# A two-layer attention block on one core: the residual is kept feature-major instead of token-major, and norm, gates and first products follow from that

## What is computed

```python
mod_x = silu(c) @ ada_w[l] + ada_b[l]          # 3*D columns: shift, scale, gate; the same for c_ctx
h  = rmsnorm(x, norm_w) * (1 + scale) + shift  # hc likewise from ctx, with c_ctx's rows
p  = h @ w_in                                  # keys, values, queries, z and g columns
o_m, o_s, o_a = three attentions (latent, windowed, axial) over x and ctx
y  = sum over b of sigmoid(g_b) * ((o_b * silu(z_b)) @ w_o_b)
x  = x + gate * (y @ w_out)                    # ctx likewise, in layer 0 only
...
return rmsnorm(x, final_norm_w)                # after both layers
```

## Time and profile before

| what | us |
|---|---|
| median of 3 runs | 2136.5 |
| profiled execution, its own time | 2135.2 |
| its span | 2133.4 |
| PE busy | 1837.2 (86%) |
| DVE busy | 1210.5 (57%) |
| ACT busy | 889.6 (42%) |
| POOL busy | 602.6 (28%) |
| start until the first projection, PE busy 48.7 | 104.0 |
| merge of layer 0, PE busy 145.6 | 172.8 |
| merge of layer 1, PE busy 79.4 | 93.9 |
| w_out of layer 1 | 46.8 |

### The profile page before, as it was taken

One profiled execution on the slowest core, in us unless ns is written; L12 is line 12 of the kernel. 1 busy time (PEld: TensorE's weight loads), 2 busy tenths in 40 slices (PEclk: granted clock), 3 DMA queues, 4 the chain that ended last, 5 costly groups with the idle time before them and its releaser, 6 DMA issues.

```text
span 2133.4 us, 27538 instructions
## 1 busy us (share of the span) xinstructions
PE 1837.2 (86%) x10845; PEld 1573.3 (74%) x10845; DVE 1210.5 (57%) x2334; ACT 889.6 (42%) x1679; POOL 602.6 (28%) x328
## 2 busy tenths in 40 slices
PE   5398998879999899998888958989869997899888
PEld 2276787768898788897767946678757886788668
DVE  1524686786666576665232342467867677676334
ACT  1222454544545455544222131344545455555332
POOL 0322221212221222113445132221303323232552
PEclk9699999989999999999999979899989999999999
DMA  6210110101111111113334112011101221122442
GB/s 213 60 46 20 31 27 22 40 11 40 51 50 41 35 35 45 30 41 113 114 103 139 60 62 58 21 34 26 34 20 50 65 65 45 39 61 60 133 138 80
DMA packets 192287, 125.90 MB, mean 59 GB/s; under 512 B 21468, under 2 KB 187934, under 8 KB 192158
## 3 DMA queue, kind: packets, MB, share of 16 engines
q1 hardware_dynamic: 187248, 108.57, 18.0%
q10 hardware_dynamic: 3630, 11.37, 1.4%
q0 software_dynamic: 1280, 4.20, 0.6%
HBM read 119.92 MB, written 4.19 MB: 58 GB/s over the span
## 4 chain that ended last, share of the span: by engine, by line
PE 66%; DVE 19%; ACT 7%; POOL 4%; issue 3%; DMA 1%; ACTq 0%; DVEq 0%; SPq 0%
PE acc L1138 50%; PE wide L1161 5%; PE ptp L1177 4%; DVE nmax L1676 3%; PE pv L1190 3%; DVE e L1693 3%; PE pv L1191 3%; POOL w_lo L1489 2%; DVE pt L1698 2%; ACT e L1402 1%; DVE k_s L1279 1%; ACT w_hi L1321 1%; DVE swapped L1588 1%; DVE rot L1589 1%; DVE q_s L1279 1%
## 5 line engine op out<-in xcount | busy, mean ns | idle before, releaser
L1489 POOL TENSOR_TENSOR w_lo<-w_raw,w_hi 128x1024 fp32r<-128x1024 f32 (+6 forms) x220 | 462.9, 2113 | 1191.3 <-ACT w_hi L1321 1191.1
L1138 PE MATMUL acc<-h_hi,w_hi 128*128 128x512 f32 (+2 forms) x1288 | 472.3, 367 | 43.1 <-POOL w_lo L1489 21.5
L1138 PE MATMUL acc<-h_lo,w_hi 128*128 128x512 f32 (+2 forms) x1288 | 468.2, 364 | 0.0
L1138 PE MATMUL acc<-h_hi,w_lo 128*128 128x512 f32 (+2 forms) x1288 | 466.5, 362 | 0.0
L1138 PEld LDWEIGHTS acc<-h_hi,w_hi 128*128 128x128 f32 (+1 forms) x1288 | 249.2, 194 | 86.0 <-issue 35.9
L1411 ACT ACTIVATE pt<-ptp 128x512 fp32r<-128x512 f32 (+3 forms) x312 | 166.2, 563 | 295.8 <-PE ptp L1177 295.2
L1138 PEld LDWEIGHTS acc<-h_hi,w_lo 128*128 128x128 f32 (+1 forms) x1288 | 248.5, 193 | 38.7 <-issue 1.5
L1138 PEld LDWEIGHTS acc<-h_lo,w_hi 128*128 128x128 f32 (+1 forms) x1288 | 249.1, 193 | 37.6 <-issue 1.3
L1676 DVE TENSOR_REDUCE nmax<-wide 128x1 f32<-128x768 f32 (+3 forms) x240 | 190.5, 794 | 130.7 <-PE wide L1161 129.1
L1321 ACT ACTIVATE w_hi<-w_raw 128x1024 fp32r<-128x1024 f32 (+6 forms) x220 | 199.8, 921 | 78.8 <-DMA w_raw<-in_w_out 67.1
L1402 ACT ACTIVATE e<-wide,nbias,rq 128x768 f32<-128x768 f32 x160 | 145.1, 907 | 172.4 <-DVE nbias L1682 171.8
(11 more groups left out here) (191 smaller groups left out, 3316.1 us busy)
## 6 DMA issues: line engine op xcount, KB each, us to landing
w_raw<-in_w_in SPq DMA_DIRECT2D x102, 512.0 KB, 3.7
w_raw<-in_ada_w SPq DMA_DIRECT2D x48, 512.0 KB, 4.3
w_raw<-in_w_out SPq DMA_DIRECT2D x16, 512.0 KB, 3.8
xres<-in_x ACTq DMA_DIRECT2D x2, 2048.0 KB, 11.2
w_raw<-in_w_o_mla SPq DMA_DIRECT2D x16, 256.0 KB, 2.8
w_raw<-in_w_o_swa SPq DMA_DIRECT2D x16, 256.0 KB, 2.8
w_raw<-in_w_o_ax SPq DMA_DIRECT2D x16, 256.0 KB, 2.8
w_raw<-in_mla_w_uq SPq DMA_DIRECT2D x16, 144.0 KB, 2.4
```

The costliest lines, as they stand in the source:

```text
L1138: ins = nc.tensor.matmul(dst, lhs, rhs, start=first, stop=last)
L1489: nc.gpsimd.tensor_tensor(w_lo[s][:, 0:k], w_raw[s][:, 0:k], f(w_hi[s][:, 0:k]), ALU.subtract).then_inc(w_lo_ready, 1)
```

## The change

The residual becomes `xt`, [128 features, 8 tiles, 768 tokens].

1. **Start.** ACT's queue issues the six input row tiles first, then the constants and the vectors. PE transposes them (XR, 8 blocks a tile), ACT and DVE copy out in turn. `xt` is saved to `x_mid` (3 MB), and the merge of each layer loads it back from there.
2. **Norm by feature tile.** ACT squares a tile (SQ, 128x768). PE sums over features by products with ones into `pv`, one product per token tile (ST; 6, before the final norm 4), for all 8 feature tiles. Then one root for all (RS), one reciprocal, 6 diagonal matrices on DVE, and a product of ones with each diagonal that spreads the factor over 128 partitions (RB, into `wide` and `pv`). Then per feature tile and group: DVE t_f = xt * mod_a * factor (HT), ACT h_hi with the shift as bias, DVE h_lo (HL). POOL has no part in it.
3. **First products in step.** `interleaved` writes four groups (ak x, ak c, ckv 0 x, ckv 0 c) into four banks, three products of each for tile k as soon as h of tile k is there (GI). ckv 1's weights are split after their read-outs.
4. **Modulation.** ada_b comes with the vectors and is added as a column; no bias DMA. All twelve j become columns; the gate too. The turning products follow one step later, in the merge between the g and the y products. Layer 0's first eight have their own raw places, eight chunks in flight. Layer 1's j 8 and 9 move from its merge to the change of layer, after w_out of layer 0.
5. **w_out by feature tile.** For t 0 to 7, 24 products of 512 (x) and 24 of 256 (ctx), with the weights as the stationary operand. The read-out is one DVE operation, xt = acc * gate column + xt. The squares and sums of the next norm follow tile by tile. At the very end `xt` is transposed back (FT), and the final norm comes after the last tile.
6. **Slots.** The merge has eight slots; w_out of layer 0 uses slots 0 to 3 and 7. Slots 4 to 7 wait for all products up to the place where the chunk was planned.

```diff
-SLOTS, TIGHT, ROOMY = 7, 3, 4
+TIGHT, ROOMY, MERGE, OUT = (0, 1, 2), (0, 1, 2, 3), (0, 1, 2, 3, 4, 5, 6, 7), (0, 1, 2, 3, 7)
+SLOTS, PLAIN, PLAIN_BASE = 8, 8, 8
...
+    def interleaved(groups):
+        last = max(c for g in groups for c in g["chunks"])
+        split_to(last)
...
+        emit("GI", gs=groups, h=n["hn"])
+        for g in groups:
+            g["read_out"]()
...
+    COLUMNS, GATES = (0, 4, 1, 5, 2, 6, 3, 7), (8, 9, 10, 11)
...
+            for tt in range(TT):
+                emit("XR", tt=tt, n=n["xt"])
+                if tt % 2 == 1:
+                    modulation()
+            for k in range(KD):
+                square(0, k)
+                if k > 0:
+                    stat(0, k - 1, range(TT))
+            modulation()
+            stat(0, KD - 1, range(TT))
+            root(0, range(TT))
+            modulation()
+            normalise(0, 0, 4)
+            modulation()
+            modulation()
+            normalise(0, 4, 6)
+            modulation()
+            run_all(tails.pop(0))
...
-        for tg in ("x", "c"):
-            go(project("ak", l, c, tg, roped=(tg == "x")))
+        interleaved([project("ak", l, c, "x", roped=True), project("ak", l, c, "c", roped=False),
+                     project("ckv", l, cks[0], "x", t=0), project("ckv", l, cks[0], "c", t=0)])
...
+        columns, gates = list(COLUMNS), list(GATES) if l == 0 else list(GATES[2:])
...
-        for j in range(D // 256):
-            cc = (chunk("wout", l, j, 0), chunk("wout", l, j, 1))
+        ups = [chunk("wout", l, t) for t in range(KD)]
+        later_ada = [ada(l + 1, j) for j in GATES[:2]] if l + 1 < LAYERS else []
+        for t in range(KD):
+            for tg in tgs:
+                go(project("wout", l, ups[t], tg, src="y", t=t, act=False, gates=gates, xl=n["xl"], needs=lambda: dict(l_done=y_ready)))
+            square(l + 1, t)
+            if l + 1 == LAYERS:
+                emit("FT", k=t, tts=tts[:2], i=0, free=n["free"], s=n["s"], pt=n["pt"])
+            if t > 0:
+                stat(l + 1, t - 1, tts)
+        for main, _ in later_ada[:1]:
+            run_all(main)
+        stat(l + 1, KD - 1, tts)
+        root(l + 1, tts)
+        if l + 1 < LAYERS:
+            run_all(later_ada[1][0])
+            for _, tail in later_ada:
+                run_all(tail)
...
+                if new(acc_done, slot_acc[c]):
+                    sp.wait_ge(acc_done, slot_acc[c])
...
-                        nc.vector.tensor_tensor(x_add[:, :], src[:, 0:256], gate[:, s, c], ALU.mult).then_inc(acc_free, 1)
-                        nc.vector.tensor_tensor(x, x, x_add[:, :], ALU.add).then_inc(xr_done, 1)
+                        nc.vector.scalar_tensor_tensor(x, src[:, 0:N], mod_col[:, 2 * KD + g["t"], s:s + 1], x, ALU.mult, ALU.add).then_inc(acc_free, 1)
```

More of the change, by code:

```diff
@@ L143, in bank, with chunk, split_to, group @@
         return turn[0]
-    def chunk(kind, *where):
+    def chunk(kind, *where, plain=False):
         chunks.append((kind,) + where)
         c = len(chunks) - 1
-        slot = min(range(usable[0]), key=lambda s: -1 if slot_last[s] is None else slot_last[s])
+        if plain:
+            slot = PLAIN_BASE + len(whole) % PLAIN
+            plain_last[slot - PLAIN_BASE] = c
+            before = [c - PLAIN] if len(whole) >= PLAIN else []
+            whole.add(c)
+        else:
+            slot = min(usable[0], key=lambda s: -1 if slot_last[s] is None else slot_last[s])
+            before = [slot_last[slot]] if slot_last[slot] is not None else [plain_last[p] for p in (slot, slot + 4) if p in plain_last and slot < 4]
+            slot_last[slot] = c
         slot_of.append(slot)
-        slot_prev.append(slot_last[slot])
-        slot_pv.append(n["pt"] if slot >= TIGHT else 0)
-        slot_last[slot] = c
-        return c
+        slot_prev.append(before)
+        slot_pv.append(n["pt"] if slot >= 3 and not plain else 0)
+        slot_acc.append(n["acc"] if 4 <= slot < SLOTS else 0)
+        return c
+    def split_to(last):
+        while n["split"] <= last:
+            emit("W", c=n["split"])
+            n["split"] += 1
     def split_ahead():
         c = n["split"]
-        known = slot_prev[c] if c < len(chunks) else c - usable[0]
-        if known is not None and (known >= held[0] or now[0] < chunk_at.get(known, 0) + LOAD_LAG):
+        known = max(slot_prev[c], default=-1) if c < len(chunks) else c - len(usable[0])
+        if known >= held[0] or now[0] < chunk_at.get(known, 0) + LOAD_LAG:
             return
-        if c <= last_used[0] + max(2, usable[0] - 2):
-            emit("W", c=c)
-            n["split"] += 1
-    def group(kind, chunk_ids=(), oldest=None, hl=False, needs=None, act=True, dve=True, cost=0, **kw):
+        if c <= last_used[0] + max(2, len(usable[0]) - 2):
+            split_to(c)
+    def group(kind, chunk_ids=(), oldest=None, hl=False, needs=None, act=True, dve=True, cost=0, at=None, **kw):
         parts = max(1, round(cost / STEP))
@@ L240, in group @@
         g["steps"] = [step(p) for p in range(parts)]
+        g["read_out"] = read_out
         return g
+    def interleaved(groups):
+        last = max(c for g in groups for c in g["chunks"])
+        held[0], last_used[0] = min(c for g in groups for c in g["chunks"]), last
+        split_to(last)
+        for b, g in enumerate(groups):
+            g.update(bank=b, n=n["acc"], before=bank_last[b], needs={}, parts=1)
+            n["acc"] += 1
+            bank_last[b] = g
+            for c in g["chunks"]:
+                chunk_last[c] = g["n"] + 1
+                chunk_at[c] = now[0]
+        emit("GI", gs=groups, h=n["hn"])
+        for g in groups:
+            g["read_out"]()
     def run_all(steps):
@@ L688, in schedule @@
                 merge += step_of(lambda: scale_table(l + 1, V_AXK))
-            merge += y_tile(l, 2, t, og)
-            if t == 0:
-                usable[0] = SLOTS
-            if t % 2 == 0:
-                merge += ada(l, GATES[t // 2])
-            if l + 1 < LAYERS:
-                merge += ada(l + 1, t)
+            gate_steps, y_steps = y_tile(l, 2, t, og)
+            merge += gate_steps
+            while tails:
+                merge += tails.pop(0)
+            merge += y_steps
+            if t == 0:
+                usable[0] = MERGE
+            due = ([(l, gates.pop(0))] if t % 2 == 0 and gates else []) + ([(l + 1, columns.pop(0))] if l + 1 < LAYERS else [])
+            for la, j in due:
+                main, tail = ada(la, j)
+                merge += main
+                tails.append(tail)
+        while tails:
+            merge += tails.pop(0)
         if l + 1 < LAYERS:
@@ L1035, in matmuls @@
                 run(a[0:g["m"], 0:size(g["tg"])], pairs)
-            elif mode in ("vs", "wout", "ada", "adaF"):
-                hi, lo = (h_hi, h_lo) if mode == "vs" else (y_hi, y_lo)
+            elif mode in ("vs", "ada", "adaF"):
+                hi, lo = h_hi, h_lo
                 for i, tt in enumerate(g.get("tts", [g.get("tt")])):
@@ L1074, in matmuls @@
                 for i in range(2):
[L1075 to L1077 removed]
+                    run(a[:, 2 * i:2 * i + 2], [(a_row[0:4, g["slot"], i * P:(i + 1) * P], sel[0:4, :])])
             return out_
```

567 lines of the change are left out of this document (310 added, 257 removed).

## The result

The changed kernel takes 2155.9 us, the median of 4 runs (2150.85 to 2160.46), against 2137.3 of the kernel before in the same comparison (2135.71 to 2138.96). The ratio is 1.0087, 95% interval 1.0062 to 1.0111: slower by 0.9%. Forecast was 2126, faster, in a range up to 2146. The profiled execution has a span of 2154.7 us, 21.3 more than before.

The account below looks back on a forecast made before the run. TensorE's products were taken as 66% of the chain, VectorE's work 19%. Terms +3.2, +5.3, -13.1, -15.6 and +9.5 sum to -10.7 us, from 2135.2 to 2124.5, or 2126 in the runs' terms; range 2104 to 2146.

Parts of the forecast that it names:

- A: Start to the end of the first projections: 3.2 us longer, ending at 134.3; bounds -7 and +12.
- The 21 that the bound gave to equal sharing: At the start, upper bound: v_rows lands at 21 us if 3 MB of loads share equally with the weights.
- The stop of 7.1: Before ckv1's products, at the start and change of layer: its weight split waits for rope read-outs, 7.1 us.
- B: Layer 0's merge: 5.3 us longer, 2.4 from later column steps and 2.9 from slot 7's later load.
- C: Layer 0's w_out to the end of the next first projections: 13.1 us shorter, 127.0 instead of 140.1.
- D: Layer 1's merge: 15.6 us shorter because gate columns 8 and 9 leave it; bounds -7 and -20.
- E: Layer 1's w_out to the end: 9.5 us longer, output products 51.3 against 46.8, then 12.8 against 8.7.
- Rival 1: Output products: statistics pull the clock down, 45 us at full price, 2171, or 2162 at four fifths; chance 0.09.
- Rival 2: Dearer start, A at +12, and VectorE queue waits in C add 6: 2141 us; chance 0.07.
- Rival 3: Layer 1's merge: stalls stay because POOL's w_lo is the limit, D only -7, 2135 us; chance 0.14.
- The rule weighed: Start: transposes don't raise the clock, so six sets run at half and leave modulation cold, some 6 us more.

Follow-up runs that it names:

- e9: The kernel before, with only the merges' turning products and gate broadcasts moved behind the next g products; 2161.2 us, ratio 1.0105.
- e3: The changed kernel with constants and vectors issued on ACT's queue ahead of the six row loads; 2152.9 us, ratio 1.0081.
- e1: The changed kernel with the merges' four turning products directly behind their modulation product again, as in the kernel before; 2149.5 us, ratio 1.0069.
- e5: The changed kernel with layer 0's output products using only slots 0 to 3, without slot 7; 2147.3 us, ratio 1.005.
- e8: The changed kernel with all the edits of e1, e2, e3, e4 and e5 together; 2110.7 us, ratio 0.9892 to the kernel before.
- e4: The changed kernel with ckv's second weights split right behind the norm's last step, ahead of the interleaved products' read-outs; 2141.2 us, ratio 1.0038.
- e11: The kernel of e8 with layer 1's gate columns 8 and 9 back in its own merge; 2129.8 us, ratio 0.9962.
- e2: The changed kernel with the final transposes of layer 1's output products one feature tile later; 2147.5 us, ratio 1.0061.
- e6: The changed kernel with sums of feature tiles 1 to 6 taken for one token tile only in both output stages; 2157.5 us, ratio 1.0102.
- e10: The changed kernel with four extra small fp32 products, result unread, behind each modulation product of the merges; 2165.3 us, ratio 1.0125.
- e13: The changed kernel with an unread copy of the turning products at their old place, the real ones late; 2164.3 us, ratio 1.0136.

## Why the prediction was wrong

**A, +3.2 forecast, +7.2 in the profile.** In the mean of seven starts it is +10.5 over the one of before, and more over the other old start (126.7, e9). The mis-sized term is the landing of the vectors, 23.5, not 17:

```profile
14.66 8.83 DMA v_rows<-in_ax_k_norm
...
45.52 14.36 PE pv L1254 x84
```

The 21 that the bound gave to equal sharing was nearer, and not enough: the issues ended at 14.66 and the last one's landing took 8.83 instead of 3.99 behind 3 MB. The seven sums took 2.05 each, near the 2.2. e3 prices the order of loads at 5 us at most. The stop of 7.1 was in the sum, and is 6.7.

**B, +5.3 forecast, +10.1.** Both mechanisms were named and each was too small: the late turning products 3.4 by e1, not 2.4, since the clock is lower behind two of the single stops; slot 7 5.0 by e5, not 2.9. Together 8.4 of the 10.1, and with both undone (e8) the stage has its 158.0 of before. The forecast had counted the second from where the last column step ended in the trace of before.

**C, -13.1 forecast, -9.2.** The pieces hold: output products of 8.5 a tile (8.59 and 8.43), sums 1.23, steps in step 18.5. The norm's start came 4 later than summed (first t_f at 92.6 after w_out's first product, not 88.2): the first two tiles' 96 products took 19.39, not 17.0, with 0.50 granted in their first 5 us, and the second modulation product 3.36, not 2.0, at 0.52. The forecast had a low clock behind the later stop only. The low clock behind the stop was as priced. The stop was accepted as a term; with its low clock it cost 7 (e4).

**D, -15.6 forecast, -12.1 by merge 1.** e11 against e8 gives 17.2 for the two gate steps alone; the late turning products give 2.6 back (e1), which the step hadn't counted in layer 1. The other 2.5 is what e11's merge, with all four gate steps, is longer than before's (93.4 and 90.9); no run explains it.

**E, +9.5 forecast, +18.4: the step that failed most.** It priced fourteen transposes at 0.137 each and no wait. The order had them directly behind the products of their own tile, and they read what VectorE writes from those products. TensorE, in order, stood 0.84 in each of seven tiles, and the first transpose took 0.33, not 0.137: 7.6 by e2. In layer 0 the sums read the tile before and wait for nothing, and so the stage held; the forecast carried that pattern over. The tail of 13.4 was forecast at 13.7 (12.8 + 0.9).

Sum: 4.0 + 4.8 + 3.9 + 3.5 + 8.9 = 25.1 on top of the forecast's -10.7, 14.4. The span grew by 21.3; the other 6.9 are the middles of the two layers (3.0 and 3.9), to which the forecast gave nothing. Both lie within what they vary by: mid 1 spans 12 us over the kernels, and e9, which has the old order there, has a middle 0 of 875.0 against 871.6 in before and 874.7 in the changed kernel. All five terms were off the same way, so E alone doesn't turn the forecast: with its wait mended the kernel takes 2147.5 (e2), still slower than before. What A, B and E have in common is a cost of order that the forecast left out or took too small, and with the orders put right the change is worth what was forecast and more (e8).

Rival 1 is refuted by e6. Rival 2 came true in part, at the start (7.2 of its 12, in the profile). Rival 3 is refuted by e11. The rule weighed, that transposes don't raise the clock, is contradicted at the start. There TensorE had done one small product (0.4 us) and then only transposes, and in e10, whose start is the changed kernel's, the second set of eight was already faster:

```profile
24.83 1.97 PE wide L1244 x8
26.80 1.33 PE ptp L1244 x8
28.13 3.55 PE acc L1209 x16
```

The same rows of the changed kernel have 1.97, 1.71 and 3.71. So the first modulation product ran nearly at its fast 3.56 and not at the 5.33 of before, where no transposes stand in front of it. Of the six sets only the first two were slow, the others took 0.87 to 1.03.

## What to carry to other kernels

When an instruction on TensorE is put behind the products whose result another engine must first read out, TensorE pays the whole read-out each time, here 0.84 us for a transpose of 0.11; put it one tile later. A stop costs its length and often, behind it, some products at a low clock (5.2 and 1.9 here). Edits that are each a clear gain in their stage (the two gate steps 17 in their merge, products in step 13 once the stop behind them is gone) can sum to a loss by five small costs of order. Each of the five stands in the order of instructions, to be read before running; mended together they turned 0.9% slower into 1.1% faster, of which some 5 us at the start are unexplained.

## What the runs showed of the hardware that was not expected

- Six 128x128 multiplications on VectorE took 1.28 with GpSimd idle for most of them, and 5.92 while it subtracted 128x1024 tiles at the same time (e6). Two of the six took 2.4 each, as long as one of those subtractions.
- The granted clock rose while TensorE did transposes, after one other small product (e10: 1.97 for the first eight, 1.33 for the next).
- Behind stops of the same length and order the granted clock was 0.50 twice and 1.00 once (changed kernel). Idle times of 1.1 to 1.2 us were followed by about 0.6 three times in e13, and of 1.3 to 1.4 by 1.00 three times in e1.
- Starts that are equal in all instructions up to the first products in step reached them 5.8 us apart (e3 at 101.9, e8 at 96.1), with 0.51 and 0.69 granted from 45 to 62 us.
- The first transpose of 128x128 after a wait took 0.33 in the chain, the next and those in a stream 0.11 (after, e2).
